# Sample states in other places, and the causal mask in the row maximum: a one-layer MLA and Mamba-2 step on Trainium2

## The reference, cut to what matters

```python
sc = (jnp.einsum('bqhr,bkr->bhqk', q_lat, ckv)
      + jnp.einsum('bqhe,bke->bhqk', q_rope, k_rope)).astype(jnp.float32) * SOFTMAX_SCALE
sc = jnp.where(k_pos[None, None, None, :] <= q_pos[None, None, :, None], sc, NEG_BIG)
p = jax.nn.softmax(sc, axis=-1).astype(ckv.dtype)
...
# sample tokens, per sequence b, head j of group g
h = jnp.exp(da_t)[..., None, None] * h + jnp.einsum('bgjp,bgn->bgjpn', x_t * dt_t[..., None], b_t)
y = jnp.einsum('bgjpn,bgn->bgjp', h, c_t)
...
mix = jnp.concatenate([o_attn, y_ssm], axis=-1)
out = x + _rmsnorm(mix @ w_out, norm_post)
```

## Time and profile before

| | us |
|---|---|
| median of 3 runs | 513.21 (512.89 to 513.52) |
| the profiled execution, in all | 512.92 |
| its span, first to last instruction | 511.1 |
| busy: TensorE, VectorE, ScalarE, GpSimd | 495.5, 352.4, 292.8, 79.5 |

### The profile page before, as it was taken

The page is one execution under the profiler, slowest core; times in us unless marked ns, Lnnn a source line. Parts: engine busy times, 40 slices in busy tenths (PEclk is TensorE's granted clock), DMA queues, the critical chain, the costliest instruction groups (busy, mean ns, idle before and its releaser), DMA issues.

```text
span 511.1 us, 12864 instructions
## 1 busy us (share of the span) xinstructions
PE 495.5 (97%) x5014; PEld 442.1 (87%) x5014; DVE 352.4 (69%) x768; ACT 292.8 (57%) x612; POOL 79.5 (16%) x100
## 2 busy tenths in 40 slices
PE   8999999999999999999999999999999999999993
PEld 7999999899999999999999865766666699999992
DVE  4843659695557675554532598699998899997643
ACT  6643412216347276553634986688986879664531
POOL 1321000000001010000000133234454302100620
PEclk9999999999999999999999999999999999999998
DMA  8642123239799999989987243663534577889712
GB/s 258 250 162 87 64 62 102 91 101 328 259 326 265 329 297 294 311 295 317 298 273 253 38 109 90 216 148 111 149 83 165 212 262 242 269 269 377 258 56 83
DMA packets 58222, 104.25 MB, mean 204 GB/s; under 512 B 7481, under 2 KB 27490, under 8 KB 58034
## 3 DMA queue, kind: packets, MB, share of 16 engines
q1 hardware_dynamic: 58162, 103.43, 61.9%
HBM read 95.75 MB, written 7.76 MB: 203 GB/s over the span
## 4 chain that ended last, share of the span: by engine, by line
PE 78%; DVE 10%; ACT 6%; issue 3%; SPq 2%; DMA 1%; ACTq 0%; DVEq 0%
PE pm L1727 17%; PE pm L1728 16%; PE pm L1729 16%; PE px L1825 3%; PE px L2025 3%; PE pm L2012 3%; PE px L1850 3%; PE pm L2044 3%; DVE w_lo L1036 2%; DVE u L1128 1%; PE px L1988 1%; PE pm L1991 1%; DMA w_raw<-in_w_in 1%; PE pm L2036 1%; PE px L2027 1%
## 5 line engine op out<-in xcount | busy, mean ns | idle before, releaser
L1727 PE MATMUL pm<-xw_hi,w_lo 128*128 128x260 f32 x544 | 158.3, 291 | 1.1 <-DVE w_lo L1207 0.9
L1728 PE MATMUL pm<-xw_lo,w_hi 128*128 128x260 f32 x544 | 153.8, 283 | 0.0
L1729 PE MATMUL pm<-xw_hi,w_hi 128*128 128x260 f32 x544 | 153.7, 282 | 0.0
L606 ACT ACTIVATE w_hi<-w_raw 128x1024 fp32r<-128x1024 f32 (+1 forms) x70 | 72.5, 1038 | 81.6 <-PE pm L1729 68.6
L1036 DVE TENSOR_TENSOR w_lo<-w_raw,w_hi 128x1024 fp32r<-128x1024 f32 (+1 forms) x70 | 85.8, 1233 | 36.7 <-ACT w_hi L606 36.7
L1727 PEld LDWEIGHTS pm<-xw_hi,w_lo 128*128 128x128 f32 x544 | 102.5, 188 | 3.6 <-issue 1.5
L1728 PEld LDWEIGHTS pm<-xw_lo,w_hi 128*128 128x128 f32 x544 | 102.4, 188 | 0.2
L1729 PEld LDWEIGHTS pm<-xw_hi,w_hi 128*128 128x128 f32 x544 | 102.4, 188 | 0.0
L1727 PE MATMUL pm<-mix_hi,w_lo 128*128 128x260 f32 x224 | 63.8, 285 | 0.1
L1729 PE MATMUL pm<-mix_hi,w_hi 128*128 128x260 f32 x224 | 63.4, 283 | 0.0
L1727 PEld LDWEIGHTS pm<-mix_hi,w_lo 128*128 128x128 f32 x224 | 42.2, 188 | 0.6 <-DVE mixlo_a L1440 0.3
(11 more groups left out here) (305 smaller groups left out, 1064.7 us busy)
## 6 DMA issues: line engine op xcount, KB each, us to landing
page<-in_cache SPq DMA_DIRECT2D x128, 288.0 KB, 4.1
w_raw<-in_w_in SPq DMA_DIRECT2D x32, 512.0 KB, 5.1
w_raw<-in_w_out SPq DMA_DIRECT2D x32, 512.0 KB, 5.3
dec<-ac_dram SPq DMA_DIRECT2D x16, 256.0 KB, 9.7
hring<-in_ssm_state SPq DMA_DIRECT2D x8, 512.0 KB, 8.1
o_ssms<-hring SPq DMA_DIRECT2D x8, 512.0 KB, 6.6
w_raw<-in_w_qb SPq DMA_DIRECT2D x6, 384.0 KB, 2.9
xraw<-in_xT SPq DMA_DIRECT2D x8, 260.0 KB, 5.1
```

Of the source, the lines that this page charges most:

```text
L606: act.activation(w_hi[s][:, 0:n], w_raw[s][:, 0:n], ACT.Copy).then_inc(a_whi, 1)
L1727: pe.matmul(out, wl, xh, start=start, stop=False)
L1728: pe.matmul(out, wh, xl, start=False, stop=False)
L1729: return pe.matmul(out, wh, xh, start=False, stop=stop)
```

## The change

Four things. The mask is no longer a product on TensorE: GpSimd sets up a 128 x 512 tile `causal` (three quarters zero, then the mask), and `mask_max` becomes one operation on VectorE that adds it to the scores, negates the sum, writes it back to PSUM and takes the row minimum; `exps` gets a scale of -1. Two quads go from attention to the projection: quads 0 to 3 stand in steps 0, 3, 4 and 5, quads 4 to 15 at items 3, 4, 6, 7 and 9 to 16. The loads of B and C and the early stores stand elsewhere on SyncE's queue. And a few calls change places (`decays(5)`, `head(5)`, `group_scale(1)`), and `orow` another address. The diff, without two hunks of addresses and semaphore names:

```diff
-STATE_DECAYS = {0: (1,), 1: (2,), 2: (3,), 3: (4,), 4: (5,)}
-DOTTED, PAIRED = [0, 0, 4, 8, 8, 12, 16, 20], [2, 3, 5, 6, 7, 8]
-ITEM_QUADS = {NIN + k: 6 + n for n, k in enumerate((3, 4, 6, 7, 9, 10, 11, 13, 14, 16))}
+STATE_DECAYS = {2: (1,), 3: (2,), 4: (3,)}
+STEP_QUADS = {0: 0, 3: 1, 4: 2, 5: 3}
+DOTTED, PAIRED = [0, 0, 4, 4, 4, 4, 8, 12], [2, 6, 7, 8]
+ITEM_QUADS = {NIN + k: 4 + n for n, k in enumerate((3, 4, 6, 7, 9, 10, 11, 12, 13, 14, 15, 16))}
...
@@ block.sync
             if t == 1:
                 sp.wait_ge(s_ssm, 16)
                 load_state(2)
-            if t == 3:
-                load_bcs(2)
-                store_state(0)
         load_ea(7)
+        load_bcs(2)
+        store_state(0)
         load_bcs(3)
         store_state(1)
         sp.wait_ge(p_y, 8)
...
         for b in range(4, NB):
             load_state(b)
-        load_bcs(4)
...
-        bc_after = {NIN + 12: 5, NIN + 15: 6, NIN + 18: 7}
+        bc_after = {NIN + 8: 4, NIN + 12: 5, NIN + 15: 6, NIN + 17: 7}
@@ block.scalar
-            if i == 11:
-                act.wait_ge(s_const, 32)
-                act.activation(mask_r, cm[:, M_MQ, :], ACT.Copy).then_inc(a_mask, 1)
-                act.wait_ge(a_mask, 1)
-                act.activation(ident_r, cm[:, M_ID, :], ACT.Copy).then_inc(a_mask, 1)
...
-            act.activation(pr[:, h % 2, i0:i0 + n], px[:, n_ % 3, 0:n], ACT.Exp, bias=nmx[:, k:k + 1], accum_out=rsum[:, k:k + 1])\
+            act.activation(pr[:, h % 2, i0:i0 + n], px[:, n_ % 3, 0:n], ACT.Exp, bias=nmx[:, k:k + 1], scale=-1.0, accum_out=rsum[:, k:k + 1])\
...
-        decays(5)
         act.wait_ge(a_dx, 1)
...
+            exps(s + 1, 3)
             if s == 0:
+                decays(5)
                 state_decay(0)
-            exps(s + 1, 3)
@@ block.vector
-            dve.tensor_reduce(nmx[:, 4 * (h % 2) + b:4 * (h % 2) + b + 1], x[:, 0:P * (b + 1)], AX.X, ALU.max,
-                              negate=True).then_inc(v_m, 1)
+            dve.tensor_tensor_reduce(x, x, causal[:, NT - w:NT], -1.0, -NEG, ALU.add, ALU.min,
+                                     nmx[:, 4 * (h % 2) + b:4 * (h % 2) + b + 1]).then_inc(v_m, 1)
...
-            if 0 < s < 6:
-                state_update(s)
+            if s and s in STEP_QUADS:
+                state_update(STEP_QUADS[s])
...
             if s == 6:
                 group_scale(0)
-                group_scale(1)
             if s == 0:
                 state_update(s)
-            if s < 6:
-                dots(s)
+            if s in STEP_QUADS:
+                dots(STEP_QUADS[s])
             gated(s)
+            if s == 6:
+                group_scale(1)
@@ block.gpsimd
+        pool.wait_ge(p_sc, NSTEP)
+        pool.memset(causal[:, 0:NT - P], 0.0).then_inc(g_mask, 1)
+        pool.tensor_copy(causal[:, NT - P:NT], cm[:, M_MQ, :]).then_inc(g_mask, 1)
@@ block.tensor
-                pe.matmul(px[:, n % 3, P * b:w], ident_r, mask_r, start=False, stop=False)
```

More of the change, by code:

```diff
@@ L226, in build @@
             dxs = at("dxs", [P, 2, 8, NB], F, o)
-            orow = at("orow", [P, 2 * P], F, o + 2048)
+            causal = at("causal", [P, NT], F, o + 512)
         if name == "ckbc":
@@ L233, in build @@
         if name == "qr":
+            orow = at("orow", [P, 2 * P], F, o)
             ys = at("ys", [P, 8, NB], F, o)
@@ L252, in build @@
     nmh, alpha, rs, epsc, nmx, rsum = (small[k] for k in ("nmh", "alpha", "rs", "epsc", "nmx", "rsum"))
-    ident_r = at("ident_r", [P, P], R, CM_ + 4 * P * M_MQ)
-    mask_r = at("mask_r", [P, P], R, CM_ + 4 * P * M_ML)
     def col(c):
@@ L285, in build @@
     s_hs0 = sem("early_states_stored")
-    a_mask, a_gf, a_out = sem("mask_rounded"), sem("group_factor_done"), sem("out_copied")
+    g_mask, a_gf, a_out = sem("mask_set"), sem("group_factor_done"), sem("out_copied")
     v_cb, a_fall = sem("cb_masked"), sem("decay_exponents_done")
@@ L1392, in dots @@
             dve.wait_ge(v_h, 4 * n + 4)
-            dve.wait_ge(v_y, PAIRED[n] if n < 6 else 8)
+            dve.wait_ge(v_y, PAIRED[n] if n < 4 else 8)
             for t in range(4 * g, 4 * g + 4):
@@ L1419, in mask_max @@
             n = 4 * h + b
-            x = px[:, n % 3, :]
+            x, w = px[:, n % 3, 0:P * (b + 1)], P * (b + 1)
+            if n == 0:
+                dve.wait_ge(g_mask, 2)
             dve.wait_ge(p_s, n + 1)
-            dve.tensor_reduce(nmx[:, 4 * (h % 2) + b:4 * (h % 2) + b + 1], x[:, 0:P * (b + 1)], AX.X, ALU.max,
-                              negate=True).then_inc(v_m, 1)
+            dve.tensor_tensor_reduce(x, x, causal[:, NT - w:NT], -1.0, -NEG, ALU.add, ALU.min,
+                                     nmx[:, 4 * (h % 2) + b:4 * (h % 2) + b + 1]).then_inc(v_m, 1)
         def inverse_sum(h, b):
@@ L1521, in _ @@
                 dve.tensor_tensor(mixlo_a[:, 0:H, NT:TT], zs, mix_hi[:, 0:H, NT:TT].bitcast(F), ALU.subtract)
-                head(5)
             if s < 6:
@@ L1526, in _ @@
                 y_pair(PAIRS[s][0])
+            if s == 0:
+                head(5)
             for h in MASKS[1].get(s, ()):
@@ L2018, in scores @@
             if h == 0:
-                pe.wait_ge(a_mask, 2)
                 pe.wait_ge(v_krl, 1)
```

## The result

The changed kernel takes 535.24 us (median of 4, 533.77 to 535.96), beside 513.37 us for the kernel before on the same chip: 1.0427 times as long, 95% interval 1.0413 to 1.0440. That is 21.9 us more. The forecast was 12.6 more, and its range ended at 533. The direction and the mechanism of the holds were right (a hold is SyncE standing at a load of B and C, with the weight loads behind it); the size was not. The profiled execution, the fastest of the four, has a span of 532.0 us, 20.9 more than before.

A forecast was written before the change was run, and what follows sets the result against it. TensorE's own instructions were taken to set the time, with VectorE nearly full. Span 511.1 - 3.3 (attention) + 15.9 (projection) = 523.7; 1.8 outside it and 0.3 to the median gave 525.8 us, range 516 to 533.

The forecast's parts named there:

- Mask products gone: TensorE in attention: 0.11 us less for each of 32 blocks, -3.5 us; -3.3 taken for attention after a VectorE charge.
- The bounds, -4.3 to -2.5: Attention's gain: -4.3 us with products and exponential waits gone in full, -2.5 with a third lost to VectorE.
- the forecast's own sign: Check on attention: the prediction is wrong if attention's end has not moved by 2.5 to 4.3 us.
- Price of the mask operation: VectorE in attention: mask in the row maximum costs +0 to +0.11 us a block, unstretched by GpSimd; 0.2 us charged.
- The fourth rival: GpSimd stretches the mask operation, attention gains nothing, landings are long: 529 to 533.6 us; chance 0.13.
- Hand-over: Attention to projection: item 1's load waits for state 1's store, costing 0 to 1.5 us; 0 taken.
- Holds: SyncE's queue in the projection: B and C loads delay items 9, 13 and 16 by +5.7, +3.4 and +3.1 us.
- The first rival: Short landings: held loads land in 3.5 to 5.4 us as the queue is empty; at 518.5 us, chance 0.20.
- The estimate of 6.0 us: Landing time of a weight load behind a B and C load, by the skill's DMA figures; the forecast took 7.0.
- The two quads: VectorE in the projection: added delays of +0.6 (items 10, 11), +0.6 (14, 15), +0.9 (17 to 19), +1.6 (20).
- Rivals 2 and 3: 2: item 9's hold isn't felt, 509.9 us, chance 0.07. 3: all holds hide, no change, 513.0 us, chance 0.05.

The follow-up runs named there:

- the repair of the queue: Loads of states 3 to 7 and item 0 ahead of bcs(3) and state 1's store: late-B-and-C-loads kernel 515.78 us, changed kernel 532.47 us.
- dots and decay late: Mask-in-row-maximum kernel with the quads of before; dots, last stack_low (VectorE) and state decay (ScalarE) moved later: 509.07 us, ratio 0.9926.
- the single hold: Kernel before, with SyncE waiting ahead of item 13's load until quad 10's dots are done: 519.13 us, ratio 1.0112.
- the states first: Changed kernel, with only the loads of states 4 to 7 put ahead of SyncE's wait for the stores of states 0 and 1: 535.75 us, ratio 1.0436.

## Why the prediction was wrong

In medians, the 21.9 us are: holds and the slow clock behind them 14.8 (535.2 to 520.4), quad 3's late place 6.0 (to 514.4), two quads more in the projection 2.4 (to 512.0), and the mask with the moved calls -1.2. The sum is 22.0. Each term is what its repair gave behind the ones before it, and in another order the terms would differ: the repair of the queue gave 4.65 us without the holds and 2.8 with them. The term of the two quads also holds the other places of the B and C loads. Point by point against the forecast's own steps, in the profiled execution, whose span was forecast at 523.7 and is 532.0:

- **Mask products gone, -3.3: mis-sized, -1.3 to the start of item 0** (1.2 to 1.4 at the end with the mask alone). The 0.11 us a product was right, and the products are gone. What failed is the step from TensorE's work to the end, "anything that makes it wait adds to the end one for one", used the other way round: the products were taken as a gain one for one. From the first score block to item 0 TensorE is busy for 84.25 us, 86.60 before, but idle for 2.84, 1.44 before; the waits for the exponential alone grew from 0.8 to 2.0 us. The bounds, -4.3 to -2.5, left out that the first block's exponential would not come any earlier. By the forecast's own sign, attention's end moving by less than 2.5 us, this step was wrong. The kernel with dots and decay late shows that the products' 3.5 us were there to be had: TensorE is busy for 83.21 us there and idle for 0.81, and the end is 4.1 us earlier.
- **Price of the mask operation, +0.11 at most: right.** At 512 columns it takes 0.69 us on the mean of 8, as the reduce did, and the accumulator read of 0.14 behind it overlaps its neighbours: with the mask alone changed, VectorE is busy for 77.03 us from the first score block to item 0, 76.09 before, which is 0.03 a block. GpSimd does not stretch it. The fourth rival needed that: its upper end, 533.6, is near the result by number only.

```profile
L1416 DVE CUSTOM_DVE_ANT_0 px<-px,causal 128x512 f32<-128x512 f32 x8 | 5.5, 691 | 2.7 <-PE px L2025 2.7
```

- **Hand-over, 0 taken of 0 to 1.5: wrong, 3.8.** The text had the dots ahead of the store of state 1 end at 393.8 and item 1 behind it. It stopped at item 1. Item 1 came when forecast (405.86 for 406.4) and cost about 0.65 us, within the forecast's 0 to 1.5. But the four state loads, which stand behind the same wait, move too, and their 2 MB lie ahead of item 2; and everything of the hand-over starts 4.5 us later. The queue was not read to its end.
- **Holds, 12.2 (5.7 + 3.4 + 3.1): right.** Measured are waits of 6.55 + 2.73 + 2.28, 11.6, and 12.1 from start to start (less the 0.12 that a product takes anyway). The landings behind a B and C load, taken as 7.0, were 7.8 (432.43 to 440.25), 6.7 (450.57 to 457.24) and 7.0 (462.57 to 469.54, by ScalarE's starts). The first rival, with 3.5 to 5.4 us, fell; the single hold shows that 3.6 us is right where no B and C load lies ahead. The estimate of 6.0 us, worked out from the Trainium skill, "DMA: Bandwidth & Descriptors", section "Specifications", is 1.2 us short of the mean of 7.2; the measurement decides. Item 18 was hidden, as forecast.
- **The clock, not in the forecast: 4.2.** No term and no rival had it, although three gaps of 3 to 6 us were forecast on an engine that had been at a clock of 1.00 throughout.
- **The two quads, 3.7 (0.6 + 0.6 + 0.9 + 1.6 at items 10 to 20): too high, about 1.8.** Counted the same way, TensorE loses 0.7 us at item 14, 0.2 at item 15 and 0.9 behind item 16. Without holds the quads cost 2.4 net. Rivals 2 and 3 needed hidden holds, and fell with them.

The three steps that failed upwards give 2.0 + 3.8 + 4.2 = 10.0, the quads take back 1.9, and 8.1 of the 8.3 us that are missing in the span are accounted for. In the median 9.4 are missing, since the median lies 1.5 us above the profiled execution and the forecast had put that at 0.3. So the error in the quads hid a part of the others.

## What to carry to other kernels

When a load with a wait of its own is moved on a queue, look up when its condition comes true at the new place and list all that stands behind it to the end, bytes included: here such waits held four weight loads, three of which TensorE felt, and put 2 MB of states in front of a load that nobody had touched. When work is taken off the engine that sets the end, name the wait that comes last there before the gain is booked: the products alone were worth 1.2 us, and the change came to 4.1 once the dots on VectorE and the state decay on ScalarE stood behind what TensorE waits for. And a new gap on TensorE is to be charged with more than its length, since the clock can fall behind it.

## What the runs showed that was not expected

- TensorE's clock fell from 1.00 to 0.50 at gaps of 6.55 and 2.28 us in the changed kernel, of 2.91 us with the single hold, of 3.93, 4.95, 4.03 and 2.15 us with the states first, and of 6.62 and 2.43 us with the queue's order repaired. It stayed at 1.00 behind gaps of 2.73 us (changed kernel, item 13) and 2.72 us (queue's order repaired, same item). So the length of a gap alone does not tell; what does is open. At item 9 it fell within the gap (0.65 from 441 to 442 us, 0.50 from 442.0 to 442.6); at item 16 it was still 1.00 from 471.0 to 471.9 and fell as the products began. In the changed kernel and with the single hold, the time at the lower clock was 3 to 5 us, a loss of 1.6 to 2.6 us each. The Trainium skill, "TensorE: Matmul & The Clock Gate", section "HAM oscillation — how this bites in real kernels", says that a wait for data can send TensorE back to half rate, and that this is paid at each such wait. By that rule, the traces agree in nine of the eleven gaps above.
- The landing of one and the same load, 512 KB, moved with what was ahead of it: 3.6 us with nothing ahead, 7.0 behind 256 KB of B and C, 6.7 and 7.8 behind that and a residual tile of 260 KB, and 9.0 and 8.8 behind 2 MB of states.
